# Summing the gate chunk of the adaLN product on VectorE instead of TensorE

## What is computed

```python
c_act = jax.nn.silu(c)                                  # c is one vector of 1024
for l in range(L):
    mod = (c_act @ w_ada[l] + b_ada[l])[:, None, :]     # 1024 x 6144 weights, one row of input
    shift1, scale1, gate1, shift2, scale2, gate2 = jnp.split(mod, 6, axis=-1)
    h = rmsnorm(x, norm1_g[l]) * (1.0 + scale1) + shift1
    u = h @ w_in[l]                                     # conv group and attention group
    ...
    y_mix = jnp.concatenate([rmsnorm(y_conv, ...), rmsnorm(y_att, ...)], axis=-1)
    x = x + gate1 * (y_mix @ w_out[l])
    h2 = rmsnorm(x, norm2_g[l]) * (1.0 + scale2) + shift2
    x = x + gate2 * hier_moe(h2, ...)                   # 16 experts
```

## Time and profile before

| | before |
|---|---|
| median of 3 runs | 645.54 us (645.4 to 645.75) |
| the profiled execution: its time | 644.83 us |
| its span in the trace | 642.9 us |
| mean granted TensorE clock | 0.948 of full |
| TensorE matmuls busy | 558.6 us, 87% of the span |
| VectorE busy | 287.0 us, 45% |
| ScalarE busy | 217.4 us, 34% |
| DMA | 189.76 MB, mean 295 GB/s |
| start of layer 1's input projection | 344.4 us, layer 0's 42.8 us |

### The profile page before, as it was taken

How to read it: one execution, slowest core, us unless ns; L and a number is a source line. 1 busy time by engine, 2 the same in 40 slices (tenths; PEclk the granted TensorE clock), 3 DMA queues, 4 the chain that set the end, 5 groups by cost and what they waited for, 6 DMA issues and landing times.

```text
span 642.9 us, 7867 instructions
## 1 busy us (share of the span) xinstructions
PE 558.6 (87%) x3148; PEld 352.8 (55%) x3148; DVE 287.0 (45%) x492; ACT 217.4 (34%) x376; POOL 13.7 (2%) x64
## 2 busy tenths in 40 slices
PE   2749999869798999999958999986976799999993
PEld 0338899445665544444426899844564654454431
DVE  4165790885247122222278496286426512222233
ACT  2064543532124522222145544264105333223120
POOL 7100000000000000000000000000000000000000
PEclk9969999988898999999998999997978699999998
DMA  8999943691299999999999737097059069999941
GB/s 266 370 389 388 402 174 131 267 409 44 73 423 408 394 364 408 413 415 412 408 387 356 250 132 261 4 405 311 1 197 389 3 259 380 417 414 414 414 187 68
DMA packets 48623, 189.76 MB, mean 295 GB/s; under 512 B 4346, under 2 KB 4426, under 8 KB 40388
## 3 DMA queue, kind: packets, MB, share of 16 engines
q1 hardware_dynamic: 47264, 185.62, 74.0%
q10 hardware_dynamic: 900, 3.23, 1.3%
q0 software_dynamic: 416, 0.32, 0.5%
HBM read 188.10 MB, written 1.05 MB: 294 GB/s over the span
## 4 chain that ended last, share of the span: by engine, by line
PE 77%; DVE 11%; ACT 5%; DMA 4%; issue 1%; SPq 1%; DVEq 0%; ACTq 0%
PE ps L1399 17%; PE ps L1213 11%; PE ps L1201 11%; PE ps L1425 9%; PE ps L1304 6%; PE ps L1379 6%; PE ps L1439 5%; DMA raw<-in_w_ada_dram 4%; PE ps L1121 4%; DVE wlo L702 2%; PE ps L1144 2%; PE ps L1294 1%; ACT work L478 1%; DVE stat L864 1%; DVE work L859 1%
## 5 line engine op out<-in xcount | busy, mean ns | idle before, releaser
L702 DVE TENSOR_TENSOR wlo<-raw,whi 128x1024 fp32r<-128x1024 f32 x64 | 74.9, 1220 | 14.0 <-ACT whi L443 13.8
L443 ACT ACTIVATE whi<-raw 128x1024 fp32r<-128x1024 f32 x64 | 64.6, 1059 | 26.0 <-PE ps L1201 10.5
L1121 PE MATMUL ps<-raw,c_rep 128*32 128x512 f32 x384 | 50.2, 660 | 17.4 <-DMA raw<-in_w_ada_dram 17.3
L1399 PE MATMUL ps<-raw,qkT 128*64 128x512 f32 x256 | 58.3, 597 | 1.6 <-ACT work L653 1.6
L1425 PE MATMUL ps<-raw,work 128*64 128x512 f32 x256 | 58.0, 598 | 0.0
L1399 PE MATMUL ps<-raw,cbc 128*64 128x512 f32 x256 | 57.2, 594 | 0.0
L1065 DVE SCALAR_TENSOR_TENSOR work<-ps,cw,work 128x256 f32<-128x256 f32 x16 | 11.0, 685 | 102.7 <-ACT work L647 102.7
L1213 PE MATMUL ps<-act_hi,whi 128*128 128x256 f32 x192 | 54.5, 284 | 0.0
L1213 PE MATMUL ps<-act_hi,wlo 128*128 128x256 f32 x192 | 54.3, 283 | 0.0
L1213 PE MATMUL ps<-act_lo,whi 128*128 128x256 f32 x192 | 54.3, 283 | 0.0
L1054 DVE TENSOR_TENSOR v_sb<-ps,gates 128x512 f32<-128x512 f32 x32 | 22.1, 691 | 64.6 <-PE ps L1425 64.6
(11 more groups left out here) (215 smaller groups left out, 850.2 us busy)
## 6 DMA issues: line engine op xcount, KB each, us to landing
raw<-in_w_ada_dram SPq DMA_DIRECT2D x48, 1024.0 KB, 9.8
raw<-in_w_gate_dram SPq DMA_DIRECT2D x64, 512.0 KB, 7.5
raw<-in_w_up_dram SPq DMA_DIRECT2D x64, 512.0 KB, 8.9
raw<-in_w_down_dram SPq DMA_DIRECT2D x32, 1024.0 KB, 10.9
raw<-in_w_in_dram SPq DMA_DIRECT2D x24, 1024.0 KB, 14.6
raw<-in_w_out_dram SPq DMA_DIRECT2D x8, 1024.0 KB, 5.4
gates<-in_b_ada_dram ACTq DMA_DIRECT2D x4, 512.0 KB, 6.5
res<-in_x_dram ACTq DMA_DIRECT2D x1, 1024.0 KB, 5.1
```

The costliest lines, as they stand in the source:

```text
L443: act.activation(whi[:, slot(n), :], raw[:, r, (i % 2) * 1024:(i % 2 + 1) * 1024], ACT.Copy).then_inc(hi_done, 1)
L702: dve.tensor_tensor(wlo[:, slot(n), :], raw[:, ring_slot[("w", l, i // 2)], (i % 2) * 1024:(i % 2 + 1) * 1024], whi[:, slot(n), :].bitcast ...
L1121: ins = pe.matmul(ps[32 * i:32 * i + 32, 6, :], c_rep[:, k, :], raw[:, ring_slot[unit], i * 512:(i + 1) * 512], start=(k == 0), stop=(k == ...
L1399: ins = pe.matmul(ps[i * SLOTS:(i + 1) * SLOTS, 0, :], hg[p // 2 % 2][:, k, c0:c0 + SLOTS], ws[i][:, :, kk, :], start=(k == 0), stop=(k == ...
```

## The change

- **G off TensorE.** The eight units of chunk G are no longer multiplied on TensorE. VectorE folds each one in (`gate_acc`): gates = unit * silu(c) + gates, one operation on 128 x 2048 elements each, the scalar being `stat[:, 40+k]`. One fold stands after the split of w_in's unit 4, one after unit 5, five after unit 11, and the eighth after `heads_out(1)`, where the first `gate_add` stood.
- **Bias.** GpSimd clears `gates` (128 x 2048) and loads the bias into partition 0 alone, two DMAs of 4 KB a layer. ScalarE's two DMAs of 512 KB are gone.
- **Sum and spread.** `ada_gate` is now a product of a matrix of ones with `gates`, which sums over the partitions and spreads the sum: half 0 after the transposes of the attention group, half 1 after the whole output projection. ScalarE (`gate_out`) copies the results back to `gates`: the first after the evacuation of the transposes, the second ahead of the scaling for the second norm. VectorE's two `gate_add` and ScalarE's `ada_out` for G are gone.
- **M moves up.** M 0,1 stands where G 0..3 stood, M 2,3 where G 4..7 stood, and M 4..7 after values(3).
- **The stream.** G's units 0 and 1 come after w_in's unit 5, the other six after unit 11; w_out's units 14 and 15 come after all of M, where they came before it. Slots of G's units are released by `gate_used`, which a fold counts up.

```diff
@@ stream
-            stream += [("w", l, u) for u in range(0 if l == 0 else 2, 12)]
-            stream += [("a", chunk_of[("G", l)], k) for k in range(KD)]
-            stream += [("w", l, u) for u in range(12, 16)]
+            stream += [("w", l, u) for u in range(0 if l == 0 else 2, 6)]
+            stream += [("a", chunk_of[("G", l)], k) for k in range(2)]
+            stream += [("w", l, u) for u in range(6, 12)]
+            stream += [("a", chunk_of[("G", l)], k) for k in range(2, KD)]
+            stream += [("w", l, u) for u in range(12, 14)]
             stream += [("a", chunk_of[("M", l)], k) for k in range(KD)]
+            stream += [("w", l, u) for u in range(14, 16)]
@@ SyncE, wait_free
-                    sp.wait_ge(ada_used, KD * l + i + 1)
+                    if chunks[l][0] == "G":
+                        sp.wait_ge(gate_used, KD * gates_before[l] + i + 1)
+                    else:
+                        sp.wait_ge(ada_used, KD * steps_before[l] + i + 1)
@@ GpSimd, at its end
+            for l in range(L):
+                if l > 0:
+                    pool.wait_ge(res_ready, l)
+                pool.memset(gates[:, :, :], 0.0).then_inc(gate_zero, 1)
+                pool.wait_ge(gate_zero, l + 1)
+                for h in range(2):
+                    c0 = (3 * h + 2) * D
+                    pool.dma_start(gates[0:1, h, :], b_ada[l:l + 1, c0:c0 + D]).then_inc(gate_bias, 16)
@@ ScalarE
+            def gate_out(l, h):
+                act.wait_ge(gate_sum, 2 * l + h + 1)
+                bank = (6, 4)[h]
+                act.activation(gates[:, h, :].rearrange("p (a b) -> p a b", a=2), ps[:, bank:bank + 2, :], ACT.Copy
+                               ).then_inc(gate_read, 1)
...
-                ada_out("G", l)
...
                 ins.then_inc(yf_ready, 1)
+                gate_out(l, 0)
...
                                ACT.Copy, scale=stat[:, 1:2]).then_inc(xn_ready[1], 1)
+                gate_out(l, 1)
                 norm_evac(m, range(2))
@@ VectorE
+            def gate_acc(l, ks):
+                if ks[0] == 0:
+                    dve.wait_ge(gate_bias, 32 * (l + 1))
+                acc = gates[:, :, :].rearrange("p g n -> p (g n)")
+                for k in ks:
+                    unit = ("a", chunk_of[("G", l)], k)
+                    dve.wait_ge(raw_full[ring_slot[unit]], landed[unit])
+                    if k > 0:
+                        dve.wait_ge(gate_used, KD * l + k)
+                    dve.scalar_tensor_tensor(out=acc, in0=raw[:, ring_slot[unit], :], scalar=stat[:, 40 + k:41 + k],
+                                             in1=acc, op0=ALU.mult, op1=ALU.add).then_inc(gate_used, 1)
...
                 split(l, 4)
+                gate_acc(l, range(0, 1))
                 split(l, 5)
+                gate_acc(l, range(1, 2))
...
                 split(l, 11)
+                gate_acc(l, range(2, 7))
...
                 heads_out(1)
-                gate_add(l, 0)
+                gate_acc(l, range(7, 8))
                 heads_out(2)
                 split(l, 14)
-                gate_add(l, 1)
@@ TensorE, ada_gate
+                    ins = pe.matmul(ps[:, bank + n, :], ones[:, :], gates[:, h, n * 512:(n + 1) * 512],
+                                    start=True, stop=True)
```

More of the change, by code:

```diff
@@ L254, in trunk @@
         chunk_of = {q: i for i, q in enumerate(chunks)}
[L255 removed]
+        steps_before = [sum(1 for kind, _ in chunks[:i] if kind != "G") for i in range(len(chunks))]
+        gates_before = [sum(1 for kind, _ in chunks[:i] if kind == "G") for i in range(len(chunks))]
         def slot(n):
```

54 lines of the change are left out of this document (25 added, 29 removed).

## The result

| | before | changed |
|---|---|---|
| median | 645.47 us (644.34 to 645.75, 4 runs) | 658.62 us (652.02 to 659.99, 4 runs) |
| the profiled execution: time, span | 644.83, 642.9 | 659.99, 658.2 |
| mean granted TensorE clock in it | 0.948 | 0.908 |

The ratio is 1.0187, 95% interval 1.0128 to 1.0246. The forecast was 647.6 with a range of 645.0 to 652.9: the direction was right, the size was not, and the range was too narrow. The four runs of the changed kernel differ by 8 us and go with the clock (652.02 at a mean clock of 0.925, 659.99 at 0.908). Out of the mean clock and the span, TensorE's clock stood at 1.2 GHz for 2 x (1 - 0.948) x 642.9 = 67 us before and for 2 x (1 - 0.908) x 658.2 = 121 us after.

What follows compares the result with a forecast made beforehand. TensorE was taken as the bound (busy 87% of the span, 77% of the chain), with room on VectorE. Layer 0's +2.7 - 2.4 + 1.1 and layer 1's +2.7 - 2.4 + 0.3 gave +2.0 us: 647.6, range 645.0 to 652.9.

Steps and rivals of the forecast that it cites:

- The slot, the queue and the landing: Attention's end: M's last load waits for the eighth fold, w_out's unit 14 behind it; `pT_out(3)` 5.2 us later, at 148.4.
- The squares, the column sum and VectorE's steps follow unchanged: Between `pT_out(3)` and the output projection: the steps up to act_lo keep their earlier durations.
- the output projection is released at 159.7: Output projection's start: set by VectorE's act_lo, 159.7 instead of 157.0, +2.7 us in each layer.
- the remaining half of M now ends near 159 and is covered: Behind values(3): M's remaining four units, 3.5 of 7.07 us, no longer set the output projection's start.
- The -2.4 us a layer: Output projection's gap: the first product with the ones keeps the clock at 2.4 GHz, making the second half 2.4 us shorter.
- The second product with the ones, +1.1 in layer 0: Behind layer 0's output projection: a 1.8 us product, less 0.6 us of earlier waiting, adds 1.1 us.
- Layer 1's +0.3: Behind layer 1's output projection: ScalarE's 1.0 us copy before the scaling, against 0.71 us of waiting, adds 0.3 us.
- Folds at 2.25 us: VectorE's folds of 2048 elements: 2.25 us each, ends 2.2 and 2.5; folds 1 to 7 covered by its waits.
- The memset: 0: Start of layer 1: GpSimd's memset beside VectorE's sums of squares taken at 0, up to 2.1 us if it delays them.
- the rivals of a fold at half rate and of the memset: Folds take 4.6 us, 663.8 us, chance 0.05; GpSimd's memset blocks VectorE in layer 1, 649.7 us, chance 0.08.
- The rival with the clock: Output projection's gap: the clock falls despite the product, 2.4 us per layer affected, 650.0 or 652.4 us; chance 0.30.
- unit 14 is not late: ScalarE's split of w_out's unit 14 needn't wait; projection released at 150.1, 628.4 us, mostly 640 to 644; chance 0.10.

Runs made afterwards that it cites:

- e_before_gap: Kernel before, plus three unread products of the ones with the mask in the output projection's gap, behind the transposes; 645.87 us (0.9975).
- e_fold7: Changed kernel with the eighth fold moved to folds 3 to 7, in front of the gated product; 637.67 us (0.988).
- e_warm: Changed kernel plus 14 unread products of the ones with the mask between probs_T(3) and the column sum; 650.19 us (1.0023).
- e_m42: Changed kernel with TensorE's chunk M as 4, 2 and, behind values(3), 2 units; 654.04 us (1.0133).
- e_f7_m42_w: Changed kernel with the eighth fold before the gated product, M as 4, 2, 2, three unread products before probs_T(3), three before the column sum; 636.92 us (0.9844).
- e_f7_m413_wr: Changed kernel, eighth fold before the gated product, M as 4, 1, 3, unread products around probs_T(3), before the logits and layer 1's places; 629.42 us (0.9717).
- e_before_gap_r: Kernel before, plus three unread products each in the output projection's gap, before the logits and before layer 1's places; 643.58 us (0.9916).

## Why the prediction was wrong

- **The slot, the queue and the landing: right.** The last load of M went out at 141.0, the two of w_out from 141.3 to 141.8, and unit 14 landed 7.03 us after its issue (7.2 to 7.4 told). With 1.7 us of later start taken off, `pT_out(3)` came at 148.6 (148.4 told). +5.4 and +5.3 us up to the column sum against +5.2.
- **"The squares, the column sum and VectorE's steps follow unchanged", so that "the output projection is released at 159.7", and "the remaining half of M now ends near 159 and is covered": wrong.** This is the step that failed first. It made 9.5 us from the column sum to the projection; 11.3 and 10.5 were measured, +1.8 and +1.0. In layer 0 the products with v and M's four units (5.18 us instead of 3.64) run at half clock and end after VectorE, so M sets the start. In layer 1 M is done in time, and of the +1.0 the clock has 0.3 (a column sum of 3.78 us instead of 3.46); the other 0.7 is `heads_out(3)`, a second wait of the projection, which the forecast did not count. Before, M ended later than both and hid it.
- **The durations of the rows taken over.** What all the clock's terms have in common: the forecast carried each stage at the clock that it had before, asked what the clock does only in the gap of the output projection, and put the input projection and the way to the experts at nothing but the product's own time. Measured were 67 and 121 us at 1.2 GHz.
- **The -2.4 us a layer: the mechanism right, the size wrong.** -0.8 and -0.9 were measured. e_before_gap gives the full 2.4 for a product in the gap. In the changed kernel the second half still had a slow piece (182.00 to 185.00 at 0.50), and so it had in e_fold7, behind the 1.96 us of idleness that the forecast had told; in e_warm and e_m42, same gap, it had none. The row on which the term rested, 120 to 124 with its clock at 1.00 in spite of idleness, did not even hold for its own place: with fewer matmuls there (0.87 of 4 us busy instead of 1.54), 124 to 130 ran at 0.50.
- **The second product with the ones, +1.1 in layer 0: right.** At the full clock it is +0.9 (21.5 us against 20.6), and e_fold7 and e_f7_m42_w, at the full clock there too, have 21.6. The kernel before took 21.8 with 3.4 us of half clock in them, so the times side by side hide it. The rest of the +5.4, some 4.5 us, is half clock in the router and the gather, which the forecast had no term for, and which e_before_gap meets without the change. Layer 1's +0.3 can't be told from the clock there.
- **Folds at 2.25 us: 2.35 alone, 12.17 for five,** and covered wherever told. **The memset: 0,** as taken. So the rivals of a fold at half rate and of the memset fell.
- **The rival with the clock had its mechanism, and a place and a price that were too small.** "The clock falls in the gap all the same" cost 2.4 us a layer at most. The clock fell at more places than the gap, and no term of the range stood for them. Filled waits gave back 8.4 us of the 13 in e_warm, with the stall in place; without it, filled waits and M as 4, 1 and 3 gave 8.3 (e_fold7 637.67, e_f7_m413_wr 629.42). Why the clock is down at one place in one kernel and up in the next stays open.
- **The rival "unit 14 is not late" was a version, not an outcome.** Its 628.4 us assumed a fold done by 129.5. e_fold7 did that. Its projection starts at 151.0 (less 0.6 us of later start) where the rival had 150.1, most of the difference being `heads_out(3)`, and its profiled execution took 631.03; the median is 637.7, as the others of its executions had a lower clock. With the clock looked after as well it is 629.4.

## What to carry to other kernels

When a change puts a wait on the path, price what is queued behind it on its engine; here that was 9.9 us a layer against the same kernel without the wait, and the forecast had 9.6 of them (`pT_out(3)` at 148.4 instead of 138.8). Then go through the stages behind and ask at which clock each row was taken, for durations read from the kernel before hold only at the clock that they had; here that was some 11 of the 13.3 us that the forecast lacked in the profiled execution. When a wait that used to come last goes, look for the next one in the code, as `heads_out(3)` here. Before moving a load in a shared ring, list for each slot who frees it and what stands behind that load in the queue and on the engine that awaits it; one fold put some 28 us earlier, at no cost, was worth 21 us by the medians. A gain by the clock at one place counts only after the whole kernel has been timed, for the same 4.8 us came and went in the kernel before.

The Trainium skill, TensorE: Matmul & The Clock Gate, under "HAM oscillation — how this bites in real kernels", tells of a kernel in which each wait for a load sends TensorE back to its low clock, so that the work after it starts slowly. The changed kernel agrees in that the column sum behind 11.66 us of waiting takes 3.78 us, where e_warm, with the wait filled, has 1.99. But the clock had fallen ahead of that wait, and e_fold7 has the same 3.78 us behind 2.66.

## What the runs showed of the hardware

**GpSimd's memset beside VectorE.** Timelines of GpSimd and VectorE in the changed kernel, where layer 1 begins:

```profile
347.24 1.80 POOL L426 MEMSET gates<- 128x2048 f32 x1 [320.13 <-DVEq L1131]
```

```profile
347.31 1.23 DVE L729 CUSTOM_DVE_ANT_0 tokmaj<-res 128x1024 f32<-128x1024 f32 x1 [0.18 <-DVEq L1131]
```

The two start 0.07 us apart, and neither waits for the other: 1.23 us is the duration in the earlier trace rows, without the memset. By the Trainium skill, GPSIMD Engine Reference, Specifications, read by itself, they would have collided; the skill's page SBUF — State Buffer, under "SBUF: two separate sides", exempts a GpSimd operation that reads no SBUF, and this trace bears that out.

**The spread.** The changed kernel's executions lie within 8 us, e_before_gap_r's within 12, with the mean clock going along each time. The kernel before lies within 1.4 us in its four runs beside the changed kernel, but the runs of it beside e_warm reach from 645.19 us at a mean clock of 0.948 to 652.25 at 0.932. Three or four runs of one kernel can thus tell less of its spread than they seem to.
